# Head norms in groups and biases added by VectorE in the first attention of a two-block network

## The chip, the cores and the metric

One core of one Trainium2 chip runs the whole kernel in one launch. The metric is the device time in microseconds, as the median of several executions. The core has TensorE (matrix products, results in eight banks of PSUM), VectorE, ScalarE, GpSimd and SyncE, each with its own program in order; they hand work to each other by semaphores.

## The reference

Two blocks of two layers each, on 512 tokens of width 1024 in float32. The change lies in the first layer, an attention with two kinds of heads:

```python
def attn_layer(h, w_in, w_out, relpos_table, q_norm_a, k_norm_a, q_norm_b, k_norm_b, sinks):
    qa, ka, va, qb, kb, vb = jnp.split(h @ w_in, cuts, axis=-1)
    qa = rmsnorm(heads(qa, H_A), q_norm_a)
    ka = rmsnorm(heads(ka, H_A), k_norm_a)
    idx = jnp.clip(rel_a, -MAX_REL_DIST, MAX_REL_DIST) + MAX_REL_DIST
    bias_a = relpos_table.astype(jnp.float32)[:, idx][:, None]
    oa = band_attention(qa, ka, heads(va, H_A), A_PREV_CHUNKS, bias_a, None)
    qb = rmsnorm(heads(qb, H_B), q_norm_b)
    kb = rmsnorm(heads(kb, H_B_KV), k_norm_b)
    bias_b = -slopes * abs(rel_b)
    ob = band_attention(qb, kb, heads(vb, H_B_KV), B_PREV_CHUNKS, bias_b, sinks)
    return jnp.concatenate([oa, ob], axis=-1) @ w_out
```

Heads are 64 wide. The eight a heads see all earlier tokens in chunks of 64 and have a bias read from a table by distance. The eight b heads share two key and value heads, see the two chunks before their own, have a bias linear in the distance (ALiBi) and a sink in the maximum and the sum. `rmsnorm` over the 64 of a head is the head norm.

## The kernel before

Activations lie transposed, features on partitions and 512 tokens along the free dimension. A weight matrix comes in slabs of 8 blocks of 128x128 (512 KB). SyncE loads a slab, ScalarE rounds it (`half`, L2054, w_hi), GpSimd subtracts for the remainder (L546, w_lo), and TensorE makes three matmuls for each block of 128x128: w_hi by xh, w_hi by xl, w_lo by xh (L725 to L727). Four slabs are in flight.

`attn_in` has 18 chunks of 128 output columns (144 blocks in all): 13 are normed (`NORMED`: queries and keys) and 5 are values (`VALUES`). The attention itself runs in 32 steps m, four query tiles t of 128 tokens for each of eight pairs of heads; the pairs 0 to 3 are b heads (ALiBi), 4 to 7 are a heads (`is_rel`). Each step has three slots f; `attn_fed` says how many blocks TensorE has done by each slot (9 in 6 slots, after 34 ahead of the steps), and `attn_at` in which slot a chunk's parts stand. The four engines walk the same grid of steps and slots.

Of a step, TensorE makes `score(m)` (two heads at once in the two halves of the array, L766, then the bias by further matmuls into the same bank: one of bf16 for ALiBi, L781; two of a Toeplitz table times the flipped identity, L774 and L776, and the mask, L778, for a heads). VectorE takes the maximum (`peak`, L1893), ScalarE the exponential (`powers`, L2456). One step later TensorE turns the probabilities (`turn`, L790) and ScalarE copies them (`copied`, L2470). Two steps later TensorE multiplies by the values (`outputs`, L809, which waits for b_ol of the step before), ScalarE scales (`weighed`, L2479, b_tok), TensorE turns the result into bank 6 (`turn_out`, L815), ScalarE rounds it (`upper`, L2486, oh) and VectorE subtracts (`low`, L1915, ol). The output projection `attn_out` then runs over all of oh and ol (L609 to L611).

A normed chunk is evicted by VectorE (`evict`, L1875), squared by ScalarE (L2436), summed over each head by a matmul with head_ones, a block matrix that also spreads the sum over the 64 rows of its head, into bank 7 (`finish`, L752); ScalarE takes the root there (L2447), VectorE the reciprocal of 128x512 (L1882) and the scaled product (L1885). A value chunk is turned through bank 7 (L748, L2444).

At the start ScalarE's queue issues the loads of the activations, the constants (cst), the bias table's rows (rel_row), the sinks and the memory tokens (m_in). The table is scaled and split in upper and lower parts (L1856, L1857, L2491, L1921), written to DRAM, and GpSimd reads it back as 128 shifted rows (`load_rel`, 16 loads of 320 KB, four heads at a time). VectorE casts masks_b, head_ones and alibi_b out of cst (L2006 to L2008), and TensorE waits for cst_ready after chunk 0.

Of the kernel before, what the change touches and what calls it, by code (L numbers as in the profile page):

```python
# [30 lines left out]
P = 128  # L31
S = 512
# [49 lines left out]
CONSTS = [("masks", 3 * P), ("head_ones", P), ("alibi", 8 * 256)]  # L82
# [73 lines left out]
def build(nc, A, out, stages=ALL):  # L156
# [4 lines left out]
    with ExitStack() as ctx:  # L161
# [60 lines left out]
        b_q = sb("b_q", [P, 6, S])  # L222
        b_k = sb("b_k", [P, 4, S])
        b_v = sb("b_v", [P, 4, S])
        b_pt = sb("b_pt", [P, 4, S])
        b_tok = sb("b_tok", [P, 2, P])
        b_stat = sb("b_stat", [P, 6, 64])
        alibi_b = sb("alibi_b", [P, 8, 256], BF16)
        head_ones = sb("head_ones", [P, P])
        sink_c = sb("sink_c", [P, 8])  # L230
        flip = sb("flip", [P, P])
        flip_r = sb("flip_r", [P, P], F32R)
        rel_h = sb("rel_h", [P, 4, 640], F32R)
        rel_l = sb("rel_l", [P, 4, 640], F32R)
        b_prob = nc.alloc_sbuf_tensor_at("b_prob", [P, 4, S], F32, offset=m_hi_at)
        cursor[0] = arena
        rel_row = sb("rel_row", [8, 767])
        rel_row_h = sb("rel_row_h", [8, 767], F32R)
        rel_row_l = sb("rel_row_l", [8, 767], F32R)
        cst = sb("cst", [P, NCST])  # L240
        rel_dram_h = nc.dram_tensor("rel_upper", [8, 767], F32R)
        rel_dram_l = nc.dram_tensor("rel_lower", [8, 767], F32R)
# [68 lines left out]
        def col(name, c=0):  # L311
# [22 lines left out]
        q_raw, q_sq, q_sum, q_root, q_rec, q_ready = (  # L334
            sem(n) for n in ("q_raw", "q_sq", "q_sum", "q_root", "q_rec", "q_ready"))
# [9 lines left out]
        cst_in, cst_ready, rel_in, rel_ready, rel_out = (  # L345
            sem(n) for n in ("cst_in", "cst_ready", "rel_in", "rel_ready", "rel_out"))
        rel_hi = sem("rel_hi")
        sink_in, flip_done = sem("sink_in"), sem("flip_done")
        rel_buf = [sem(f"rel_buf{h}") for h in range(4)]
# [23 lines left out]

        def attn_fed(x):

            return min(18 * KD, 34 + 9 * (x + 1) // 6) if x >= 0 else 34

        def attn_at(c, extra):

            x = 0  # L380
            while attn_fed(x) < min(KD * (c + 1) + extra, 18 * KD):
                x += 1
            return x + (1 if KD * (c + 1) + extra > 18 * KD else 0)

        def step_bank(m, half):

            return bank[2 + 2 * (m % 2) + half]

        VALUES = (1, 8, 11, 14, 17)
        NORMED = [c for c in range(18) if c not in VALUES]  # L390
        UNITS = {}

        def norm_slot(c):
# [2350 lines left out]
```

## Time and profile before

| | us |
|---|---|
| median of 3 runs | 3249.08 |
| lowest and highest | 3249.03, 3249.24 |
| the profiled execution | 3255.58 |
| its span, first to last instruction | 3253.7 |
| TensorE busy | 3085.4 (95%) |
| VectorE, ScalarE, GpSimd busy | 1516.7, 1305.3, 1186.2 |

The profile is of one execution, which took 6.5 us more than the median. "Busy" is the time in which an engine had an instruction; matmuls are pipelined and overlap in the record. Where a row has an idle time in brackets, the name behind the arrow is what released the instruction. PEclk is the clock granted to TensorE, 1.00 for 2.4 GHz and 0.50 for 1.2 GHz. The attention lies between 13.5 and about 343 us of the span, its output projection included.

### The profile page before, as it was taken

The page shows a single profiled execution, that of the slowest core. Times are in us where ns is not written, and L with a number is a line of the kernel's source. Part 1 is how long each engine was busy: PE and PEld are TensorE (multiplying, and loading weights), DVE is VectorE, ACT ScalarE, POOL GpSimd, SP SyncE. Part 2 cuts the span into 40 slices and gives each one's busy share as a digit, 9 for nine tenths or more (in the row PEclk, how much of TensorE's full clock was granted, in tenths as well). Part 3 has the DMA queues.
Part 4 walks back from the last instruction along what each step waited for, and adds up shares of the span by engine and source line. Part 5 has one row for each costly group of instructions (what it writes and reads, how often), then busy time and mean ns, then how long its engine had stood idle before and what let it go on. Part 6 is the DMA issues. An engine that isn't in the chain of part 4 may idle for free.

```text
span 3253.7 us, 40002 instructions
## 1 busy us (share of the span) xinstructions
PE 3085.4 (95%) x13798; PEld 2401.8 (74%) x13798; DVE 1516.7 (47%) x2136; ACT 1305.3 (40%) x2061; POOL 1186.2 (36%) x511
## 2 busy tenths in 40 slices
PE   6899999998998899999999999999989999899998
PEld 4566788876675578888866777888867787778886
DVE  5542555327615744553269534332257763333222
ACT  4663444333335534443322534443233343344432
POOL 3121444443342034444432532444432254144443
PEclk9997999999998999999999999999999999999999
DMA  4120323332220022323311322323321132122232
GB/s 151 39 78 22 95 90 97 97 99 75 84 91 7 1 72 91 96 90 100 101 59 59 117 72 60 95 91 96 102 79 59 59 117 85 45 91 92 95 97 90
DMA packets 74459, 263.18 MB, mean 81 GB/s; under 512 B 8664, under 2 KB 8928, under 8 KB 74096
## 3 DMA queue, kind: packets, MB, share of 16 engines
q1 hardware_dynamic: 68400, 249.07, 24.6%
q10 hardware_dynamic: 3648, 7.46, 0.6%
q0 software_dynamic: 2304, 5.24, 0.6%
q8 instruction: 65, 1.06, 0.1%
q14 instruction: 42, 0.34, 0.0%
HBM read 259.59 MB, written 2.15 MB: 80 GB/s over the span
## 4 chain that ended last, share of the span: by engine, by line
PE 45%; issue 34%; POOL 14%; DVE 5%; ACT 2%; DMA 0%; POOLq 0%; ACTq 0%; DVEq 0%; SPq 0%
POOL w_lo L546 14%; PE bank L609 11%; PE bank L610 11%; PE bank L611 11%; PE bank L1108 1%; PE bank L1056 1%; PE bank L1057 1%; PE bank L1058 1%; DVE bank L1882 1%; PE bank L1238 1%; DVE bank L1786 1%; PE bank L1241 1%; PE bank L685 0%; PE bank L725 0%; PE bank L726 0%
## 5 line engine op out<-in xcount | busy, mean ns | idle before, releaser
L546 POOL TENSOR_TENSOR w_lo<-w_raw,w_hi 128x1024 fp32r<-128x1024 f32 x475 | 1144.8, 2412 | 1891.2 <-ACT w_hi L2054 1891.2
L2054 ACT ACTIVATE w_hi<-w_raw 128x1024 fp32r<-128x1024 f32 x475 | 501.1, 1056 | 724.9 <-DMA w_raw<-w_glu_out 156.7
L609 PE MATMUL bank<-xh,w_hi 128*128 128x512 f32 x1864 | 745.5, 400 | 18.0 <-POOL w_lo L546 13.4
L610 PE MATMUL bank<-xl,w_hi 128*128 128x512 f32 x1864 | 740.8, 397 | 0.0
L611 PE MATMUL bank<-xh,w_lo 128*128 128x512 f32 x1864 | 740.4, 397 | 0.0
L609 PEld LDWEIGHTS bank<-xh,w_hi 128*128 128x128 f32 x1864 | 352.1, 189 | 113.2 <-POOL w_lo L546 19.5
L610 PEld LDWEIGHTS bank<-xl,w_hi 128*128 128x128 f32 x1864 | 352.1, 189 | 86.3 <-issue 1.7
L611 PEld LDWEIGHTS bank<-xh,w_lo 128*128 128x128 f32 x1864 | 352.2, 189 | 85.9
L1343 DVE TENSOR_TENSOR xt<-bank,xt 128x512 f32 x72 | 49.8, 692 | 505.6 <-PE bank L611 505.6
L611 PE MATMUL bank<-hh,w_lo 128*128 128x512 f32 x704 | 279.1, 396 | 0.0
L609 PE MATMUL bank<-hh,w_hi 128*128 128x512 f32 x704 | 279.1, 396 | 0.0
L610 PE MATMUL bank<-hl,w_hi 128*128 128x512 f32 x704 | 279.1, 396 | 0.0
L1969 DVE TENSOR_TENSOR f_u<-bank,rstd 128x512 f32<-128x512 f32 x88 | 60.9, 691 | 274.2 <-PE bank L611 274.2
L2547 ACT ACTIVATE hh<-f_h 128x512 f32 x88 | 55.6, 632 | 257.8 <-DVE f_h L1972 257.8
L610 PEld LDWEIGHTS bank<-hl,w_hi 128*128 128x128 f32 x704 | 132.6, 188 | 32.3
L609 PEld LDWEIGHTS bank<-hh,w_hi 128*128 128x128 f32 x704 | 132.6, 188 | 32.3
L611 PEld LDWEIGHTS bank<-hh,w_lo 128*128 128x128 f32 x704 | 132.6, 188 | 32.3
L1972 DVE TENSOR_TENSOR f_h<-f_y,f_u 128x512 f32<-128x512 f32 x88 | 150.7, 1712 | 8.5 <-DVE f_u L1969 2.7
L1786 DVE SCALAR_TENSOR_TENSOR bank<-c_u,cols,bank 128x512 f32<-128x512 f32 x192 | 130.3, 750 | 12.7 <-PE bank L1108 12.2
L1317 DVE TENSOR_TENSOR acc<-acc,sq 128x512 f32<-128x512 f32 x88 | 102.3, 1163 | 71.1 <-ACT sq L2045 71.1
L609 PE MATMUL bank<-oh,w_hi 128*128 128x512 f32 x320 | 129.9, 406 | 2.6 <-DVE ol L1840 2.1
L610 PE MATMUL bank<-ol,w_hi 128*128 128x512 f32 x320 | 128.3, 401 | 0.0
(341 smaller groups left out, 4660.0 us busy)
## 6 DMA issues: line engine op xcount, KB each, us to landing
w_raw<-w_ffn_in SPq DMA_DIRECT2D x88, 512.0 KB, 3.5
w_raw<-w_glu_in SPq DMA_DIRECT2D x88, 512.0 KB, 3.5
w_raw<-w_ffn_out SPq DMA_DIRECT2D x48, 512.0 KB, 3.5
w_raw<-w_glu_out SPq DMA_DIRECT2D x48, 512.0 KB, 3.5
w_raw<-w_ssm_in SPq DMA_DIRECT2D x41, 512.0 KB, 3.5
w_raw<-w_pw SPq DMA_DIRECT2D x24, 512.0 KB, 3.5
w_raw<-w_diff_in SPq DMA_DIRECT2D x24, 512.0 KB, 3.5
w_raw<-w_attn_in SPq DMA_DIRECT2D x18, 512.0 KB, 3.5
```

The lines of the kernel that those rows point to most:

```text
L546: pool.tensor_tensor(w_lo[:, slot, :], w_raw[:, slot, :], w_hi[:, slot, :].bitcast(F32), ALU.subtract).then_inc(w_split, 1)
L609: pe.matmul(b, wh, hi[:, k, 0:n], start=(k == 0), stop=False)
L610: pe.matmul(b, wh, lo[:, k, 0:n], start=False, stop=False)
L611: mm = pe.matmul(b, wl, hi[:, k, 0:n], start=False, stop=last)
L1056: pe.matmul(b, wh, hi[:, k, 0:n], start=(k == 0), stop=False)
L1317: dve.tensor_tensor(acc[:], acc[:], sq[:, j % 2, :], ALU.add).then_inc(x_acc, 1)
L1343: dve.tensor_tensor(row(xt, c), b[:], row(xt, c), ALU.add).then_inc(bank_free, 1)
L1786: ins = dve.scalar_tensor_tensor(conv_bank(p)[:], c_u[:, p % 4, k:k + S], col("dw_w", CONVW * p + k), conv_bank(p)[:], ALU.mult, ALU.add)
L1969: dve.tensor_tensor(f_u[:], bu[:], rstd[:], ALU.mult).then_inc(bank_free, 1)
L1972: dve.tensor_tensor(f_h[:], f_y[:], f_u[:], ALU.mult).then_inc(f_prod, 1)
L2054: act.activation(w_hi[:, slot, :], w_raw[:, slot, :], ACT.Copy).then_inc(w_half, 1)
L2547: act.activation(row(hh, p), f_h[:], ACT.Copy)\
```

## The change

- The 13 normed chunks form seven groups (`GROUPS`). `sums` makes a thin result: for each chunk of a group two rows (one a head) of 32 in bank 7, with a selection matrix `pick`. ScalarE takes the root of 32x512 into acc, VectorE the reciprocal in two halves of 256 columns, in two slots, and `spread` brings it back to 128 rows of bank 7 by a matmul over 32 rows with `heads`.
- The blocks are fed 40 ahead of the steps and then 5 in 4 slots, so that they last into step 27 instead of step 24. The order of the chunks is k, q, v, q.. instead of k, v, q.. at the head.
- The biases are no longer matmuls. `peak` is one VectorE operation per head, which adds the bias (rel_t or alibi_b) in the bank and takes the maximum with the sink as its floor. rel_t comes ready made from the host for all eight heads (128x640 each); GpSimd loads it, one head a slab, scales it by 8 and adds the mask.
- Bank 7 is shared by sums, spreads, value transposes and output transposes in one order (`SHARED`), each waiting for the release of the one before. Outputs are turned, rounded and subtracted once for each pair (128x512) instead of once for each step.
- Buffers for all keys, queries and values, so that no eviction waits for scores. The load of m_in moves from the start to the first feed-forward layer.

```diff
+        VALUES = (2, 8, 11, 14, 17)
+        GROUPS = ((0, 1), (3, 4), (5,), (6, 7), (9, 10), (12, 13), (15, 16))
+        EARLY = (8, 8, 8, 4, 4, 4, 4)
+        SLOT0 = len(EARLY)
         def attn_fed(x):
-            return min(18 * KD, 34 + 9 * (x + 1) // 6) if x >= 0 else 34
+            if x < SLOT0:
+                return sum(EARLY[:x + 1])
+            return min(18 * KD, sum(EARLY) + 5 * (x - SLOT0 + 1) // 4)
...
+        def turn_step(m):
+            return m + 1
+        def output_step(m):
+            return m + 2
+        def group_slot(g):
+            return attn_at(GROUPS[g][-1]) + 1
+        def shared_bank():
+            events = []
+            for g, chunks in enumerate(GROUPS):
+                events.append((group_slot(g), 0, "sums", g))
+                events += [(group_slot(g) + 3 + (i if g else 0), 1, "spread", c) for i, c in enumerate(chunks)]
+            events += [(attn_at(c) + 1, 2, "values", c) for c in VALUES]
+            events += [(slot_of(output_step(NT * pair + NT - 1), 2), 3, "output", pair) for pair in range(8)]
+            return sorted(events)
...
+            def attn_stream(st):
+                for c in range(st.chunks):
+                    if 3 <= c < 11:
+                        pool.dma_start(rel_t[:, c - 3, :], A["rel_t"][c - 3]).then_inc(rel_in[c - 3], 16)
+                    if 6 <= c < 14:
+                        h = c - 6
+                        pool.wait_ge(rel_in[h], 16)
+                        if h == 0:
+                            pool.wait_ge(cst_ready, 2)
+                        pool.tensor_scalar(rel_t[:, h, :], rel_t[:, h, :], 8.0, None, ALU.mult).then_inc(rel_done, 1)
+                        pool.wait_ge(rel_done, 2 * h + 1)
+                        pool.tensor_tensor(rel_t[:, h, S:], rel_t[:, h, S:], masks_b[:, 0, :], ALU.add).then_inc(rel_done, 1)
+                    lower_half(st.slab0 + c)
...
-                    pe.matmul(bank[7][:], head_ones[:], sq[:, 0, :], start=True, stop=True).then_inc(q_sum, 1)
+                def sums(g):
+                    for i, c in enumerate(GROUPS[g]):
+                        pe.wait_ge(q_sq, NORMED.index(c) + 1)
+                        pe.matmul(bank[7][0:32, :], pick[:, 30 - 2 * i:62 - 2 * i], sq[:, i, :], start=(i == 0),
+                                  stop=(c == GROUPS[g][-1]), skip_group_check=True).then_inc(q_sum, 1)
+                def spread(c):
+                    g, i = place_of(c)
+                    pe.wait_ge(q_rec, 2 * g + 2)
+                    pe.matmul(bank[7][:], heads[:, i * P:(i + 1) * P], acc[0:32, :], start=True, stop=True).then_inc(q_bc, 1)
...
+                def output(pair):
+                    pe.wait_ge(b_otok, NT * (pair + 1))
+                    for t in range(NT):
+                        mm = pe.transpose(bank[7][:, t * P:(t + 1) * P], b_tok[:, t, :], ident[:])
+                    mm.then_inc(b_ot, 1)
...
                     if m:
-                        pe.wait_ge(b_ol, m)
+                        pe.wait_ge(b_otok, m)
...
+                def inverse(g, part):
+                    dve.wait_ge(q_root, g + 1)
+                    r = acc[0:32, part * 256:(part + 1) * 256]
+                    dve.reciprocal(r, r).then_inc(q_rec, 1)
...
-                        top = dve.reduce_max(b_stat[:, 0, u:u + 1], step_bank(m, half)[:, 0:nk], AX_X)
+                        top = dve.tensor_tensor_reduce(b, b, bias, 1.0, floor, ALU.add, ALU.max, b_stat[:, 0, u:u + 1])
...
+                def rooted(g):
+                    act.wait_ge(q_sum, normed_in(g + 1))
+                    if g:
+                        act.wait_ge(q_bc, normed_in(g))
+                    act.activation(acc[0:32, :], bank[7][0:32, :], ACT.Sqrt, scale=1.0 / 64, bias=eps[0:32, 0:1])\
+                        .then_inc(q_root, 1)
...
-                dve.tensor_copy(head_ones[:], cst[:, 3 * P:4 * P]).then_inc(cst_ready, 1)
-                dve.tensor_copy(alibi_b[:], cst[:, 4 * P:].rearrange("p (a n) -> p a n", a=8)).then_inc(cst_ready, 1)
+                dve.tensor_copy(pick[:], cst[:, 3 * P:3 * P + 64]).then_inc(cst_ready, 1)
+                dve.tensor_copy(heads[:].rearrange("p (a n) -> p a n", n=64),
+                                ident[0:32, 0:8].unsqueeze(2).broadcast_to([32, 8, 64])).then_inc(cst_ready, 1)
...
+                if s == "ffn0":
+                    act.dma_start(m_in[:], A["memt"]).then_inc(m_landed, 16)
...
-            act.dma_start(m_in[:], A["memt"]).then_inc(m_landed, 16)
```

## Rows read from the trace of the kernel before

**Rows 1.** stretches of the first attention: us from:to, length, busy (x) by engine, clock, DMA

```profile
13.50:57.80 44.30, 32.56 (x114) 22.49 (x114) 30.64 (x30) 19.15 (x26) 19.11 (x14) 0.92 0.51 169
57.80:241.70 183.90, 163.43 (x849) 116.36 (x849) 94.09 (x206) 112.54 (x295) 37.52 (x22) 0.95 0.17 52
241.70:252.60 10.90, 8.62 (x54) 5.60 (x54) 3.17 (x11) 5.24 (x20) 0.00 (x0) 1.00 0.12 46
252.60:298.00 45.40, 39.67 (x164) 30.06 (x162) 8.30 (x27) 15.29 (x52) 0.00 (x0) 0.54 0.00 1
```

**Rows 2.** timeline of the start, ScalarE and its queue: start, us, engine, line, operation

```profile
7.47 0.45 ACTq L2562 DMA_DIRECT2D m_in<-memt  x1
...
8.03 1.28 ACT L2054 ACT_TABLE_LOAD   x1 [8.03 <-issue]
```

**Rows 3.** timeline around the constants' casts, GpSimd and TensorE

```profile
23.48 5.22 POOL L546 TENSOR_TENSOR w_lo<-w_raw,w_hi 128x1024 fp32r<-128x1024 f32 x2 [10.66 <-ACT w_hi L2054]
...
29.97 0.79 PE L725 MATMUL bank<-xh,w_hi 128*128 128x512 f32 x1 [4.64 <-DVE alibi_b L2008]
```

**Rows 4.** timeline ahead of the first scores, ScalarE and TensorE

```profile
51.93 1.06 ACT L2054 ACTIVATE w_hi<-w_raw 128x1024 fp32r<-128x1024 f32 x1 [6.15 <-DMA w_raw<-w_attn_in]
...
57.78 0.59 PE L766 MATMUL bank<-b_k,b_q 64*128 64x128 f32 x4 [4.99 <-DVE b_q L1885]
```

**Rows 5.** timeline of TensorE in a step with no norm chain

```profile
124.63 0.39 PE L781 MATMUL bank<-alibi_b,ident_b 128*128 128x256 bf16 x2
...
124.78 0.48 PE L725 MATMUL bank<-xh,w_hi 128*128 128x512 f32 x1
...
126.26 0.60 PE L748 MATMUL bank<-ident,sq 128*128 128x128 f32 x4
...
126.69 1.00 PE L809 MATMUL bank<-b_v,b_pt 128*128 128x64 f32 x8
...
127.51 0.48 PE L725 MATMUL bank<-xh,w_hi 128*128 128x512 f32 x1
```

**Rows 6.** timeline of a step with a norm chain, TensorE and VectorE

```profile
150.31 1.02 PE L752 MATMUL bank<-sq,head_ones 128*128 128x512 f32 x2
...
151.17 0.60 PE L790 MATMUL bank<-ident,b_prob 128*128 128x128 f32 x4
...
152.06 3.37 DVE L1882 RECIPROCAL bank<-bank 128x512 f32<-128x512 f32 x1 [4.52 <-ACT bank L2447]
...
156.47 1.10 PE L809 MATMUL bank<-b_v,b_pt 128*128 128x64 f32 x8 [1.38 <-DVE ol L1915]
```

**Rows 7.** timeline of TensorE in two steps with no projections, around their biases

```profile
242.36 0.38 PE L774 MATMUL bank<-rel_h,flip_r 128*128 128x256 f32 x1
...
243.13 1.95 PE L809 MATMUL bank<-b_v,b_pt 128*128 128x64 f32 x16
...
246.88 0.45 PE L774 MATMUL bank<-rel_h,flip_r 128*128 128x384 f32 x1
...
247.88 0.61 PE L809 MATMUL bank<-b_v,b_pt 128*128 128x64 f32 x4
```

**Rows 8.** timeline of the tail: an exponential, the last scores, the first output projection

```profile
248.88 0.58 ACT L2456 ACTIVATE b_prob<-bank,b_stat 128x384 f32<-128x384 f32 x1 [2.54 <-DVE b_stat L1897]
...
278.95 2.08 PE L766 MATMUL bank<-b_k,b_q 64*128 64x512 f32 x4
...
297.97 0.77 PE L609 MATMUL bank<-oh,w_hi 128*128 128x512 f32 x1
```

**Rows 9.** groups by line and shape, VectorE: count, busy us, mean ns, idle before

```profile
L1736 DVE RECIPROCAL rstd<-rstd 128x256 f32<-128x256 f32 x8 | 13.8, 1738 | 1.3 <-ACT rstd L2331 1.3
...
L1763 DVE TENSOR_TENSOR bank<-bank,rstd 128x512 f32<-128x512 f32 x8 | 5.5, 693 | 18.2 <-PE bank L1058 18.2
...
L1893 DVE TENSOR_REDUCE b_stat<-bank 128x1 f32<-128x512 f32 x8 | 5.3, 689 | 7.6 <-PE bank L778 7.6
...
L1515 DVE TENSOR_SCALAR a_stat<-a_stat 128x1 f32<-128x1 f32 x64 | 9.8, 154 | 2.2
```

More of the change, by code:

```diff
@@ L344, in build @@
             sem(n) for n in ("a_score", "a_max", "a_exp", "a_prob", "a_turn", "a_pt", "a_pv", "a_oh", "a_ol"))
[L345 to L349, printed above, removed]
+        cst_in, cst_ready, sink_in, sink_ready, rel_done = (
+            sem(n) for n in ("cst_in", "cst_ready", "sink_in", "sink_ready", "rel_done"))
+        rel_in = [sem(f"rel_in{h}") for h in range(8)]
         def score_bank(n, peers):
@@ new lines, in build, with released, place_of @@
+        SHARED = shared_bank()
+        def released(k):
+            _, _, kind, n = SHARED[k]
+            if kind == "sums":
+                return q_root, n + 1
+            if kind == "spread":
+                return q_ready, NORMED.index(n) + 1
+            if kind == "values":
+                return v_ready, 2 + VALUES.index(n) + 1
+            return b_ol, n + 1
+        def place_of(c):
+            g = next(i for i, chunks in enumerate(GROUPS) if c in chunks)
+            return g, GROUPS[g].index(c)
@@ L391, in build, with normed_in @@
+        def normed_in(groups):
+            return sum(len(chunks) for chunks in GROUPS[:groups])
         UNITS = {}
@@ new lines, in output, with events @@
+                def output(pair):
+                    pe.wait_ge(b_otok, NT * (pair + 1))
+                    for t in range(NT):
+                        mm = pe.transpose(bank[7][:, t * P:(t + 1) * P], b_tok[:, t, :], ident[:])
+                    mm.then_inc(b_ot, 1)
+                use = {"sums": sums, "spread": spread, "values": values, "output": output}
+                def events(x):
+                    for k, (at, _, kind, n) in enumerate(SHARED):
+                        if at == x:
+                            pe.wait_ge(*(released(k - 1) if k else (nrm_root, nrm[0])))
+                            use[kind](n)
@@ L757, in score @@
                     if t == 0:
[L758 removed]
+                        pe.wait_ge(q_ready, NORMED.index(7 + 3 * (pair - 4)) + 1 if is_rel(m) else 2 + pair)
                     if m >= 2:
@@ L1865, in evict @@
                             dve.wait_ge(v_turned, v)
+                        dve.wait_ge(q_sum, sum(n < c for n in NORMED))
                         dst = sq[:, 1, :]
```

345 lines of the change are left out of this document (134 added, 211 removed).

## Prediction

> **What bounds the kernel now.** The change touches only the first attention, so I read that stage first in stretches [rows 1], then the waits by line, then the timelines of single steps. The stage has four parts. From 13.5 to 57.8 us the first three and a half weight chunks run alone, and 34 of 144 projection blocks (a block is three matmuls of 512 columns) are done. From 57.8 to 241.7, the steps 0 to 24 carry the other 110 blocks. From 241.7 to 298.0, the steps 25 to 33 have no block left, and then the output projection starts [rows 8]. In the second part TensorE is busy 163.4 of 183.9 us: 20.5 are idle, and a granted clock of 0.95 means that a tenth of the time ran at 1.2 instead of 2.4 GHz, which costs 9.2. So its work there is 154.2 us at 2.4 GHz, and 29.7 are lost. In the last part the clock is 1.00 up to 252.6 and 0.54 after it: TensorE had been busy 8.6 of 10.9 us before it fell. The stage is bound by TensorE's work and, around it, by waits that cost time twice, as idle and as clock.
>
> The waits have a pattern. In a step with a head norm, VectorE's reciprocal of 128x512 takes 3.37 us, and VectorE works in order: behind it stand the scaling, the small subtraction into ol and the maximum. TensorE's weighted sums wait 1.38 us for that ol [rows 6]. In a step without a norm TensorE has no gap [rows 5]. There are eleven such chains in the steps and thirteen in all.
>
> **The front, to the first scores.** ScalarE's first work starts at 8.03 us, just behind its own queue's last issue, the load of m_in at 7.47 [rows 2]. The change takes two issues out of that queue (m_in, moved to ffn0, and rel_row), up to 1.0 us earlier (the m_in issue is 0.45, the other is taken alike), nothing if the first weights had only just landed. In ffn0 the issue stands behind the norm's root, where VectorE's 3.37 us reciprocal covers it; uncovered it would cost 0.45. TensorE then waits until 29.97 for the constants' casts, which share the time with two GpSimd subtractions of 5.22 us together [rows 3]. The cast of head_ones becomes one of 64 columns, and a copy into heads (32x512) is added, at most 0.7 by the 128x512 rows. GpSimd now goes on to its third slab without the wait for rel_out; if a cast has to wait for that subtraction too (5.22/2 = 2.6 us), it costs that. Of the two together I take -0.5, bounds -1.0 and +2.6. The old front lost 6.15 us on a slab that landed at 51.93, behind the burst of sixteen 320 KB bias loads, and TensorE then stood 4.99 us before the scores [rows 4]. The new loads are eight, one for each slab, so I take no such wait (bound: the 6.15 stay). What takes its place is the work: 40 blocks instead of 34 (6 x 0.74 = 4.4, from 1.48 us for two blocks [rows 5]), one more spread pair (2 x 0.86 [rows 6]), one wait between the two spreads (scaling and hand-over, 0.9). Two sums and one set of value transposes stand in the front as now. So score 0 starts at 57.8 - 0.5 - 5.0 + 4.4 + 2.6 = 59.3, against 57.8 now.
>
> **The steps with projections.** Part by part, at 2.4 GHz, from the 154.2 us:
> - Six blocks fewer (110 to 104): -4.4.
> - Biases leave TensorE. For an ALiBi step they take 0.15 (124.63 to 124.78) [rows 5], 16 times 2.4. For a relative step 0.77 with 256 keys and 1.00 with 384 [rows 7], so by the same slope 0.54 and 1.23 with 128 and 512, 3.54 for a pair; two pairs and step 24 give 7.6. Together -10.0.
> - Output transposes: 23 single ones, about 0.1 each (a quarter of 0.43, 126.26 to 126.69), become six groups of four, 0.43 each: 0.
> - Sums: thinner output, the same 512 columns in. No row shows a 32-wide result; the bounds are 0.22 and 0.86, and I take the 0.86 of [rows 6], so 0.
> - Spreads are new: 11 matmuls of 32x512 in these steps, at 0.86: +9.5. The lower end is half of that.
> - Three more steps (25 to 27) come into this part. TensorE was busy 8.6 us in two of them, less 1.8 of bias, and half as much again for the third: about +9.
>
> Sum 158.3 us. On it come the stalls. The eleven chains with a 3.37 us reciprocal become six with two of 1.74 (128x256 [rows 9]; 32 rows save nothing, since the time goes with the columns), placed in different slots, with the spread three slots after the sum. From the end of the sums: root and hand-over 0.9 (151.17 to 152.06 [rows 6]), up to 1.3 for its table (the length of a table load [rows 2] is in that stretch hidden by the wait), 1.74 twice, so 4.4 to 5.7 us. Three slots of TensorE's work (158.3/28/3 = 1.9 each) give 5.7 less the slot's share that lies before the sums, so about 1.2 of stall for each group, 7 in all. The weighted sums now wait for b_otok (ScalarE) and not for ol (VectorE), so nothing on TensorE waits behind the reciprocal but the spreads. Behind the reciprocals on VectorE stands the next maximum, up to 1.7 late; its exponential is wanted by TensorE more than a slot later. Five more for the other waits and some low clock: 12, bounds 3 (almost none) and 29.7 (as much as now). GpSimd gets sixteen more operations, at most 8 x (1.6 + 0.3) us from its 2.6 for 1024 columns; it waits most of the stage, and its slabs are wanted 18 blocks later, so 0. So step 28 starts at 59.3 + 170.3 = 229.6.
>
> **VectorE's bias and maximum in one.** No row has that operation. The nearest are the maximum (0.689 for 512 columns) and an addition from bank to bank (0.693) [rows 9]. Bounds for 512 columns are 0.69 (one pass) and 1.38 (two); I take 0.75, and 0.15 for handing out the maximum, the price of the 128x1 row. That is 0.2 more for each half than now, 0.4 for a step, while one of three small operations of the ALiBi steps goes. VectorE is busy 94 of 184 us [rows 1], so this costs only where the step is a chain, at the end. The Trainium skill, VectorE: DVE Perf Modes, section "Two Vector instructions with no wait between them", says that an operation with an accumulator output is two instructions, the main one and a read of the accumulator. No row here shows one on VectorE; by it the 0.15 is an instruction of its own, and by a single one the tail below would be about 1 us shorter.
>
> **The end.** Only the steps 28 to 31 and the two behind them have no blocks. Steps 25 and 26 now take 4.3 and 5.1 us at 2.4 GHz, with ScalarE waiting 2.54 us for the maximum [rows 8]. Bias out (0.8) and VectorE's extra (0.4) nearly cancel; steps 28, 29, 30 at 3.6, 4.3 and 5.1 give 13.0. Step 31 to the output projection takes 19.0 now, at 1.2 GHz (278.95 to 297.97 [rows 8]); bias goes (2.2 at that clock) and the ol wait goes (0.9), VectorE's extra and the four transposes cost 1.1: 17. I let the clock fall again, in step 30: +1. The tail is 31, bounds 25 (the clock stays) and 40 (it falls at once and VectorE takes two passes).
>
> **Sum.** The output projection starts at 229.6 + 31 = 260.6 instead of 298.0: -37.4 us. What follows is the same program. The profiled execution took 3255.6 with a span of 3253.7, and the median of the runs is 3249.1; I apply the difference to both: 3218.2 for such an execution, and 3211.7 for the median.
>
> **Rivals.**
> - Almost no stall is left and the spreads cost half: stalls 3 instead of 12, spreads -5, tail 27: 9 + 5 + 4 = 18 less, 3194. For it: steps without a norm have no gap now. Against: the shared bank. Chance 0.13.
> - The shared bank takes the reciprocal's place. Sums, spreads, value and output transposes all use bank 7 in one order, and TensorE stands in order at each. There are 33 such uses. If they cost 0.7 us each on average instead of what I allow, the stalls are about 30 and with their clock the result is about 3230. For it: a chain of 4.4 to 5.7 us per group, with TensorE behind it. Against: three slots are left for it. Chance 0.2.
> - Slower. The same place, the handing on of bank 7: at 33 uses the gain of 37 plus the 7 already counted is used up at 44/33 = 1.3 us each. At 2 us each it is 66 - 44 = 22 slower, 3271. The longest wait of TensorE for a norm now is 4.99, and eleven chains with all else cost 29.7, so this needs more loss from six groups than eleven give now. Chance 0.04.
> - It does not do what it says: the stage stays bound as now, because the steps' stalls stay near 30 and the tail runs wholly at 1.2 GHz (40), and the front loses 2.6 more. 37 - 18 - 9 - 3 = 7 of gain are left, 3242; with VectorE dearer, within 0.2%. Chance 0.06.
>
> **Numbers.** The forecast has 0.57 (3201 to 3222). The range reaches into the first two rivals: 3195 to 3230. A measurement of this kernel can tell about 0.2%, 6.5 us. Faster 0.93, same 0.03, slower 0.04.
>
> **What would show it.** Right: score 0 near 59.3 and no wait for a slab ahead of it; steps of some 6.1 us; reciprocals of 1.74, fourteen of them; no wait of the weighted sums for ol; blocks up to step 27; the output projection at 261. Wrong: TensorE waiting before spreads or sums by more than 2 us a group; a bias-and-maximum above 1 us for 512 columns; a low clock before step 28; the first block after the casts later than 32.

## The result and the profile after

The changed kernel takes 3229.11 us, the median of 5 runs (3225.24 to 3234.08), against 3249.03 for the kernel before beside it (5 runs, 3242.79 to 3249.24). The ratio is 0.9944, 95% interval 0.9929 to 0.9958: 18 us faster by the ratio, 20 by the two medians. The forecast was 37.4 us faster (3211.7), with 3230 as the slow end of its range. The direction came out; the size is about half, at the slow end of that range.

The profile after is of an execution of 3225.24 us (span 3223.4), the fastest of the five. Its stage in stretches, as [rows 1]: up to the first scores, up to step 28, and up to the output projection. Columns as there: from:to, length, busy time of TensorE, its weight loads, VectorE, ScalarE and GpSimd, the granted clock, and the DMA columns.

```profile
13.50:59.97 46.47, 39.13 (x133) 25.95 (x131) 28.06 (x28) 17.75 (x25) 22.87 (x15) 0.93 0.35 115
59.97:237.29 177.32, 163.18 (x818) 108.19 (x817) 81.78 (x242) 102.45 (x286) 47.04 (x29) 0.98 0.15 45
237.29:266.05 28.76, 22.72 (x125) 18.50 (x125) 6.16 (x27) 12.07 (x40) 1.13 (x1) 0.72 0.06 19
```

Score 0 starts at 59.97 us (59.3 forecast), step 28 at 237.29 (229.6), the output projection at 266.05 (260.6; [rows 8] have 297.97). What a stretch loses to the clock is its length times what the clock lacks to 1.00: 177.3 x 0.02, some 3.5 us; added up from short windows, as all such losses below, it is 3.4. So the steps hold 163.2 - 3.4 = 159.8 us of work at 2.4 GHz, 14.1 idle and 3.4 of clock. 158.3 of work was forecast and 12 for the other two together.

The start and the casts, timeline of the same kernel, as [rows 2, 3]:

```profile
6.94 1.28 ACT L2091 ACT_TABLE_LOAD   x1 [6.94 <-issue]
...
22.38 5.22 POOL L564 TENSOR_TENSOR w_lo<-w_raw,w_hi 128x1024 fp32r<-128x1024 f32 x2 [10.66 <-ACT w_hi L2091]
22.87 2.53 DVE L2041 CAST masks_b<-cst 128x384 bf16<-128x384 f32 x1
25.32 2.33 DVE L2042 COPY pick<-cst 128x64 f32<-128x64 f32 x1
```

ScalarE begins 1.1 us earlier, as both issues out of its queue promised (up to 1.0). VectorE's operations, by line and shape (count, busy us, mean ns, idle before), as [rows 9]:

```profile
L1911 DVE RECIPROCAL acc<-acc 32x256 f32<-32x256 f32 x14 | 24.0, 1726 | 14.6 <-ACT acc L2481 14.6
L1946 DVE CUSTOM_DVE_ANT_0 bank<-bank,alibi_b,sink 128x256 f32<-128x256 f32 x24 | 10.5, 479 | 11.7 <-PE bank L828 11.7
L1946 DVE DVE_READ_ACCUMULATOR2_ANT b_stat<- 128x1 f32 x64 | 8.9, 140 | 0.0
...
L1946 DVE CUSTOM_DVE_ANT_0 bank<-bank,rel_t 128x512 f32<-128x512 f32 x8 | 5.4, 715 | 12.3 <-PE bank L828 12.3
```

Fourteen reciprocals of 32x256 take 1726 ns each, close to what the 1738 of [rows 9] for 128x256 said. The bias and maximum in one take 715 ns for 512 columns and 140 for the accumulator (0.75 and 0.15 taken). The Trainium skill, VectorE: DVE Perf Modes, section "Two Vector instructions with no wait between them", says that an operation with an accumulator output is two instructions; this trace agrees, with 64 reads of 140 ns in rows of their own.

What TensorE waited for between 55 and 300 us (total, times, longest):

```profile
PE bank L828 <- ACT b_pt L2521: 10.1, 11, 3.0
PE bank L793 <- DVE acc L1911: 6.1, 4, 3.1
PE bank L804 <- ACT b_tok L2531: 1.3, 2, 0.7
```

L793 is `spread`, waiting for the reciprocals; L828 `score`, waiting for the last probabilities' copy. Inside the steps (up to 237.3) the first of the three is 6.3 us in nine waits and the second is whole. No matmul of L856, the weighted sums, waits for VectorE any more, as [rows 6] had it for L809. The tail of the changed kernel, timeline of TensorE, as [rows 8]:

```profile
250.40 2.08 PE L828 MATMUL bank<-b_k,b_q 64*128 64x512 f32 x4 [3.01 <-ACT b_pt L2521]
...
256.53 2.79 PE L856 MATMUL bank<-b_v,b_pt 128*128 128x64 f32 x12 [0.88 <-ACT b_pt L2521]
...
265.31 1.09 PE L804 MATMUL bank<-ident,b_tok 128*128 128x128 f32 x4 [0.70 <-ACT b_tok L2531]
266.05 0.78 PE L655 MATMUL bank<-oh,w_hi 128*128 128x512 f32 x1
```

### The profile page after: what moved, and what is told of

Same layout as the page of the kernel before. It is cut to its first block, busy times and chain, and to the rows that moved or that the text cites. A ratio compares the mean times of both kernels' runs of the same rounds, so it can differ in the third digit from the quotient of the medians.

```text
span 3223.4 us, 39788 instructions
## 1 busy us (share of the span) xinstructions
PE 3068.6 (95%) x13696; PEld 2381.8 (74%) x13696; DVE 1499.1 (47%) x2159; ACT 1285.8 (40%) x2020; POOL 1199.1 (37%) x517
## 3 DMA queue, kind: packets, MB, share of 16 engines
q8 instruction: 64, 1.05, 0.1%
## 4 chain that ended last, share of the span: by engine, by line
PE 45%; issue 34%; POOL 14%; DVE 4%; ACT 2%; POOLq 0%; ACTq 0%; DMA 0%; DVEq 0%; SPq 0%
POOL w_lo L592 14%; PE bank L655 11%; PE bank L656 11%; PE bank L657 11%; PE bank L1144 1%; PE bank L1092 1%; PE bank L1093 1%; PE bank L1094 1%; PE bank L1274 1%; PE bank L771 1%; DVE bank L1822 1%; PE bank L772 1%; PE bank L773 1%; PE bank L731 1%; DVE acc L1911 0%
## 5 line engine op out<-in xcount | busy, mean ns | idle before, releaser
L592 POOL TENSOR_TENSOR w_lo<-w_raw,w_hi 128x1024 fp32r<-128x1024 f32 x457 | 1100.6, 2410 | 1760.0 <-ACT w_hi L2091 1760.0
L655 PE MATMUL bank<-xh,w_hi 128*128 128x512 f32 x1864 | 745.3, 400 | 18.8 <-POOL w_lo L592 14.2
```

What stands on the lines that cost most here:

```text
L592: pool.tensor_tensor(w_lo[:, slot, :], w_raw[:, slot, :], w_hi[:, slot, :].bitcast(F32), ALU.subtract).then_inc(w_split, 1)
L655: pe.matmul(b, wh, hi[:, k, 0:n], start=(k == 0), stop=False)
```

## The experiments

All ratios are to the kernel before, run beside each kernel. "Spread" is L793, "idle" and "clock" are what TensorE loses in a stretch; its "work" is its busy time less the clock's loss.

**Both kernels again.** One profile of each is thin ground for a difference of 20 us.

> The kernel before, unchanged, for a second profile. Between the two profiles at hand the output projection of the first attention starts 32 us earlier after the change (298.0 to 266.0) and the spans differ by 30, but the medians differ by 20. Theory A, the first profile of before was an unusual execution: its low clock inside the first attention (five falls of 3.4 us in the steps, 48 us in the tail) is more than usual; then this profile shows fewer falls, a projection start of 286 to 292 us, and a time near 3245 to 3249. Theory B, the attention always gains 32 and the rest of the program gives some back after the change: then this profile shows a start near 298 again with a span near its own median, so 6 us less behind 298 than the first profile had (2955.7). The ratio to itself is 1.000 within 0.2%.

> The changed kernel, unchanged, for a second profile; its first one came from its fastest execution (3225.2, others up to 3234.1). Theory A, low clock inside the attention differs by execution: a slower profile shows its extra time ahead of 266 us, with more falls of the clock there. Theory B: the start of the output projection stays at 266 within 1 us, and the extra time lies behind it. Ratio to before 0.994 within 0.002.

Before: 3247.37 us (12 runs, 3242.7 to 3254.81), ratio 0.9998 [0.9988, 1.0008]. After: 3228.22 (5 runs, 3226.69 to 3237.75), ratio 0.9950 [0.9938, 0.9963]. The spread within one program goes with the clock: over the whole span the changed kernel had 0.977 at 3226.69 and 0.974 at 3237.75, the one before 0.977 at 3242.70 and 0.974 at 3254.81. A clock of 0.003 less is 10 us of such a span. Stretches of the new profile of before (up to score 0, to step 25, to the output projection), then of the changed kernel (to score 0, to step 28, to the output projection):

```profile
13.50:57.30 43.80, 31.98 (x112) 22.04 (x112) 30.65 (x30) 19.15 (x26) 19.08 (x14) 0.96 0.54 171
57.30:241.34 184.04, 163.41 (x849) 116.58 (x849) 94.16 (x206) 112.57 (x295) 37.50 (x22) 0.95 0.18 52
241.34:292.46 51.12, 43.41 (x215) 32.78 (x216) 11.33 (x38) 20.39 (x72) 0.00 (x0) 0.71 0.03 10
```

```profile
13.50:60.51 47.01, 39.06 (x134) 25.80 (x132) 27.97 (x27) 17.70 (x25) 22.88 (x15) 0.93 0.35 115
60.51:244.65 184.14, 170.82 (x818) 113.07 (x817) 80.42 (x242) 102.96 (x286) 47.07 (x29) 0.94 0.14 43
244.65:271.45 26.80, 20.75 (x124) 16.42 (x125) 6.16 (x27) 12.09 (x40) 1.13 (x1) 0.81 0.06 20
```

Of the two theories the first fits for the kernel before: its second profile starts the output projection at 292.5. Three things follow. First, the tail of before is 51.1 us here and 56.3 in [rows 1]: its clock came back to 1.00 for 10 us in between (0.71 over the tail against 0.54 in the last row of [rows 1]). The forecast took its tail from one execution, 6.5 us above the median, that had the worse case. Second, from the start of the output projection to the end the program is the same but for the load of m_in, and it took 2955.7 and 2953.5 us in the two profiles of before and 2957.3 and 2953.5 in the two of the change: it moves by 4 us by itself, so a difference of a few us between two profiles isn't yet one between two kernels. Third, the changed kernel's steps take 184.1 us with the clock at 0.94 and 177.3 at 0.98, with the same waits (13.3 and 14.1 us idle). Where the low clock lay in the slower of these two, the one just shown:

```profile
67.40:70.60 3.20, 0.16 (x1) 0.00 (x0) 3.20 (x3) 1.03 (x1) 0.82 (x2) 0.94 0.15 62
70.60:80.40 9.80, 9.74 (x19) 4.42 (x20) 3.76 (x15) 2.55 (x8) 5.11 (x4) 0.50 0.12 33
...
118.00:124.80 6.80, 6.80 (x20) 4.61 (x20) 2.33 (x6) 2.19 (x9) 2.00 (x2) 0.50 0.10 20
138.50:141.90 3.40, 3.40 (x16) 3.00 (x15) 0.66 (x6) 1.59 (x8) 1.62 (x2) 0.50 0.00 0
```

TensorE was nearly idle from 67.4 to 70.6 (the spread of the first group in the steps, 3.10 us), and then ran at 1.2 GHz for 9.8 us, busy throughout. At 118.0 the waits ahead were short (0.71 us in the step before), and the other profile, with the same wait (0.72), had no fall there. Behind the wait of 3.10 us both profiles have a low clock, one for 10 us and the other for 7. The Trainium skill, TensorE: Matmul & The Clock Gate, section "A second HAM failure mode: psum-queue depth-cycling", says that in a bf16 kernel which cycles through its PSUM banks, short idles between groups of matmuls make the clock go up and down. The falls at 118.0 and 138.5, behind waits of 0.71 and 1.72 us, are of that kind, and their absence in the other profile is not explained by it; no run here changes how the banks are used.

**Fewer blocks a slot alone, in the kernel before.** Does the longer cover of the steps pay by itself?

```diff
-            return min(18 * KD, 34 + 9 * (x + 1) // 6) if x >= 0 else 34
+            return min(18 * KD, 34 + 8 * (x + 1) // 6) if x >= 0 else 34
```

> The kernel before with one part of the change alone: its 110 blocks in the steps go 8 to 6 slots instead of 9 to 6, so that they last into step 27 instead of 24. My sum has the three later steps without blocks as the tail's gain, mostly by the clock: before, 45 us run at 0.54. If the low clock of the tail is the main thing that the change removes, this alone gives 8 to 15 us (ratio 0.995 to 0.9975), and the tail from step 28 is about 31 to 35 us. If the tail is bound by its chain, blocks moved there only fill gaps: also a gain, but of the idle in the steps 25 to 27, 2 to 5 us (0.9985 to 0.9995).

3238.61 us, ratio 0.9971 [0.9962, 0.9981]: 9 us. Its stretches, to step 28 and to the output projection:

```profile
57.19:249.84 192.65, 171.39 (x923) 121.03 (x923) 97.97 (x221) 118.98 (x322) 37.41 (x22) 0.98 0.17 50
249.84:280.79 30.95, 25.83 (x142) 19.41 (x143) 6.47 (x23) 13.02 (x45) 0.00 (x0) 0.77 0.04 16
```

Steps 0 to 27 and the tail together take 223.6 us instead of 235.2. Nearly all of that is clock: 11.1 us are lost instead of 23.5 (3.9 in the steps and 7.2 in the tail, against 8.5 and 15.0), while the idle is 26.4 instead of 28.3. The steps are as idle as before (21.3 us against 20.6), and still lose less than half as much to the clock.

**The reciprocal alone, and the biases alone, in the kernel before, and both.** The change shortens the chain and takes the biases off TensorE; which of the two pays?

```diff
-                    dve.reciprocal(bank[7][:], bank[7][:]).then_inc(q_rec, 1)
+                    dve.reciprocal(bank[7][:, 0:256], bank[7][:, 0:256]).then_inc(q_rec, 1)
```

```diff
-                        pe.matmul(step_bank(m, half)[:, 0:nk], q, k, start=True, stop=False, skip_group_check=True)
...
-                            pe.matmul(b[:, 0:nk], ident_b[:], alibi_b[:, 4 * half + pair, 256 - nk:256], start=False, stop=True,
-                                      skip_group_check=True).then_inc(b_score, 1)
+                        pe.matmul(step_bank(m, half)[:, 0:nk], q, k, start=True, stop=True, skip_group_check=True)\
+                            .then_inc(b_score, 1)
```

> The kernel before with the head norms' reciprocal taken over 256 of 512 columns (the other half is left at the root, so the second half of the tokens is scaled wrongly; same instructions otherwise). It halves the one instruction that I named as the source of the stalls: 3.37 to 1.74 us, 13 times, 21 us in all, 11 of them in the steps. In the two profiles of before the steps 0 to 24 take 184.0 us with 20.6 idle and 8.5 lost to the low clock. If VectorE's reciprocal is what TensorE waits for, at least half of the 18 us goes from the steps: idle near 11, ratio 0.995 to 0.997. If the waits come from elsewhere in the in-order chain (ScalarE's part, table loads), idle falls by under 3 and the ratio is above 0.9985.

> The kernel before without its bias matmuls (biases and masks are left out of the scores; all loads stay). My sum took 10.0 us of TensorE's work out of the steps 0 to 24 and some 7 at the low clock out of the tail. If TensorE's work is the bound, the steps are 10 us shorter and the start of the output projection 14 to 17 us earlier: ratio 0.9945 to 0.996. If the steps are bound by chains, idle takes the place of the work, work falls by 10 but the steps by under 5: ratio above 0.9975.

> The kernel before with the bias and mask matmuls left out and the reciprocal over 256 of its 512 columns (half of the tokens keep the root instead of its inverse; the biases are missing from the scores, so nothing that comes after is the reference's). Apart, the first gave 4 us and the second 16. If the work that leaves TensorE is worth nothing while chains through VectorE and ScalarE set the steps, and is worth its length once they are shorter, the two together give more than 20: some 27, ratio 0.9910 to 0.9925. If the clock takes what the work gives (an emptier engine falls to 1.2 GHz more often), they give 20 or less: 0.9935 to 0.9955.

| left out of the kernel before | us | ratio | gain |
|---|---|---|---|
| half of each reciprocal | 3230.78 | 0.9951 [0.9937, 0.9966] | 16 |
| all biases and masks on TensorE | 3242.98 | 0.9985 [0.9975, 0.9996] | 3 to 5 |
| both | 3222.36 | 0.9920 [0.9903, 0.9936] | 25 |

The steps 0 to 24 and the tail, first with half reciprocals, then without biases, then with neither:

```profile
56.53:224.42 167.89, 157.56 (x849) 113.92 (x849) 78.10 (x206) 112.23 (x295) 37.52 (x22) 0.98 0.19 57
```

```profile
56.89:235.42 178.53, 155.51 (x763) 109.97 (x763) 94.32 (x206) 112.71 (x295) 37.45 (x22) 0.95 0.18 54
235.42:284.12 48.70, 39.93 (x174) 29.62 (x174) 10.87 (x38) 20.50 (x72) 0.00 (x0) 0.61 0.03 10
```

```profile
55.49:216.15 160.66, 147.69 (x763) 105.31 (x763) 78.22 (x206) 112.18 (x295) 37.52 (x22) 0.99 0.21 60
```

Halving the reciprocal takes 16.2 us off the steps without touching TensorE's work: idle 20.6 to 10.3, clock 8.5 to 3.4. Each of the eleven norms loses 1.6 us of reciprocal (3.37 to 1.77), 17.6 us in all, so rather more than half of what VectorE saves was idle of TensorE, and the clock gave 5.1 on top. The weighted sums' wait for ol, which the prediction had named, falls from 6.1 to 0.6 us in the steps; the output transposes' wait for b_tok, which it had not, stays (6.8 to 6.3). Taking 8.7 us of work out of the steps gave 5.5 (178.5 against 184.0); idle grew by 2.4 and the clock's loss by 0.8. In the tail some 7 us of work went and 2.4 of time: the clock there was 0.61 instead of 0.71. I had expected more of the biases (a miss). With half reciprocals under it, the same removal is worth 8 to 10 us by the medians (3230.78 to 3222.36), but the intervals of the two, 1 to 8 and 3 to 17 us, overlap widely, and by the profiles it is the same: the output projection starts 8.3 us earlier without the biases (292.5 to 284.1) and 8.7 earlier with half reciprocals under it (272.9 to 264.2). The idle grows alike as well, by 2.4 and by 2.7 us. So it isn't shown that removed work is worth more once the chain is shorter. The 27 us that I had worked out for both was 25.

**The spreads one slot later, in the changed kernel.** If TensorE waits at L793 for the reciprocal, a later spread should find it done.

```diff
-                events += [(group_slot(g) + 3 + (i if g else 0), 1, "spread", c) for i, c in enumerate(chunks)]
+                events += [(group_slot(g) + (4 if g else 3) + (i if g else 0), 1, "spread", c) for i, c in enumerate(chunks)]
```

> The changed kernel with the spreads of all groups but the first one slot later (four after the sums instead of three). I priced a group's stall before the spread at 1.2 us; the profiles show 3.1, 0.98, 0.72, 0 to 0.4 and 1.34: 6.5 in all, and a fall of the clock of 7 to 10 us behind the first. If the spread is too early, the first wait becomes 1.5 or less and the others go: idle less by 4 to 5, and the clock does not fall at 70 us: ratio 0.991 to 0.9935. If VectorE's reciprocals only move with the slots, nothing changes: 0.9945 to 0.9955.

3220.07 us (3219.45 to 3222.05), ratio 0.9917 [0.9899, 0.9935]: 8 us better than the change. TensorE's waits for the reciprocal, and the steps:

```profile
PE bank L793 <- DVE acc L1911: 2.4, 1, 2.4
```

```profile
60.06:231.85 171.79, 162.83 (x817) 108.50 (x817) 81.82 (x241) 102.20 (x286) 47.94 (x29) 0.98 0.15 46
```

Four waits of 6.1 us became one of 2.4; the steps take 171.8 us, idle 9.0 and clock 3.4. Against the slower of the two profiles of the change, 4.3 us of idle and 8.3 of clock are gone; against the faster 5.1 and nothing. Two signs of the expectation missed: the first wait is 2.4 us and not 1.5 or less, and the clock is still low behind it, from about 72 to 80 us.

**Half reciprocals in the changed kernel.** The same wait, from its other side.

```diff
-                    r = acc[0:32, part * 256:(part + 1) * 256]
+                    r = acc[0:32, part * 256:part * 256 + 128]
```

> The changed kernel with each reciprocal of the head norms over 128 of its 256 columns (half of the tokens keep the root instead of its inverse). If what the spreads wait for is the reciprocals' own length, as the waits of 3.10, 0.98, 0.71 and 1.36 us before spreads say, they shrink by 1.74 each where they are that long (0.87 times 2), the steps become some 4 us shorter and the clock falls less often: as good as the spreads one slot later, ratio 0.991 to 0.993. If the spreads wait for something else that VectorE does first, it stays at 0.9945 to 0.9955.

3221.74 us, ratio 0.9923 [0.9906, 0.9940]. The steps:

```profile
61.11:233.41 172.30, 162.93 (x818) 108.13 (x817) 72.67 (x242) 102.58 (x286) 47.06 (x29) 0.98 0.14 46
```

172.3 us, idle 9.4, clock 3.5: shortening the reciprocal and moving the spread away from it do the same. The wait is the reciprocals'. It is 1.5 us here, once, and the clock behind it is low as before (71 to 80 us): what brings that fall, in every profile of the changed kernel, stays open.

**ScalarE copies the probabilities ahead of its norm work.** The other large wait, scores for b_pt, might go if ScalarE did that copy first in its slot.

```diff
+                        for j in range(BM):
+                            if f == 1 and turn_step(j) == m:
+                                copied(j)
...
-                            if f == 1 and turn_step(j) == m:
-                                copied(j)
```

> The changed kernel with one order changed on ScalarE: in a step's middle slot the copy of the turned probabilities comes before that slot's squares and roots, not after. In both profiles of after, TensorE stands 1.0 to 1.7 us before the scores of steps 5, 11, 19 and 24 for that copy, which stands behind a square that waits for VectorE's eviction of a chunk that TensorE has only just finished. I priced no such wait. If this is the cause, these waits go: 4 to 5 us of idle in the steps (of 13.7), and the falls of the clock behind them (at 118 and 138 us in the second profile) become rarer: ratio to before 0.991 to 0.9935 against 0.995 of the change. If the square is late instead and holds the sums, the waits only move: ratio 0.994 to 0.996.

3241.35 us (10 runs, 3238.57 to 3245.11), ratio 0.9985 [0.9975, 0.9995]: 11 to 13 us slower than the change, where I had expected it faster. One group's chain, timeline of ScalarE, VectorE and TensorE, in the changed kernel run again, and then with the copy ahead:

```profile
83.50 0.66 PE L837 MATMUL bank<-ident,b_prob 128*128 128x128 f32 x4
...
84.11 0.68 ACT L2481 ACTIVATE acc<-bank,eps 32x512 f32<-32x512 f32 x1
...
84.82 1.74 DVE L1911 RECIPROCAL acc<-acc 32x256 f32<-32x256 f32 x1 [3.07 <-ACT acc L2481]
...
87.66 1.73 DVE L1911 RECIPROCAL acc<-acc 32x256 f32<-32x256 f32 x1
...
89.54 1.09 PE L793 MATMUL bank<-acc,heads 32*128 32x512 f32 x2 [0.98 <-DVE acc L1911]
```

```profile
84.31 0.65 PE L837 MATMUL bank<-ident,b_prob 128*128 128x128 f32 x4
...
84.79 0.66 ACT L2521 ACTIVATE b_pt<-bank 128x256 f32<-128x256 f32 x2 [1.65 <-PE bank L837]
85.47 1.28 ACT L2481 ACT_TABLE_LOAD   x1
86.76 0.68 ACT L2481 ACTIVATE acc<-bank,eps 32x512 f32<-32x512 f32 x1
...
87.47 1.74 DVE L1911 RECIPROCAL acc<-acc 32x256 f32<-32x256 f32 x1 [5.10 <-ACT acc L2481]
...
90.32 1.73 DVE L1911 RECIPROCAL acc<-acc 32x256 f32<-32x256 f32 x1
...
92.19 2.04 PE L793 MATMUL bank<-acc,heads 32*128 32x512 f32 x2 [3.40 <-DVE acc L1911]
```

As the kernel has it, ScalarE loads the root's table (82.81 to 84.09) while TensorE still makes the sums, and takes the root 0.6 us after TensorE's next matmul starts (84.11 after 83.50). With the copy ahead, the copy waits for the transposes (84.79), the table load of 1.28 stands behind it in the open, and the root comes 2.45 us after (86.76 after 84.31). The spread waits 3.40 instead of 0.98. TensorE's waits between 55 and 300 us, and the steps:

```profile
PE bank L793 <- DVE acc L1911: 10.5, 5, 3.4
PE bank L828 <- ACT b_pt L2521: 7.0, 8, 3.0
```

```profile
61.12:255.14 194.02, 177.38 (x817) 116.69 (x816) 83.16 (x241) 103.51 (x286) 48.18 (x29) 0.90 0.13 41
```

The scores' wait shrank by 2 to 3 us and the spreads' grew by 4.3. There are as many table loads as before (six for the root and seven for the exponential in the steps), so it is their place and not their number. Idle is 16.6 instead of 13.3, but the clock is 0.90 and takes 18.5 instead of 11.7: of the 9.9 us that the steps are longer, two thirds are clock.

**Dummy matmuls in the tail of the changed kernel.** What does the low clock at the end cost? Eight matmuls in each of the steps 28 to 32, into a bank that nobody reads.

```diff
+                def fill(n):
+                    pe.wait_ge(bank_free, BANKS + st.chunk0 + 17)
+                    for _ in range(n):
+                        pe.matmul(bank[0][:, P:4 * P], ident_b[:], masks_b[:], start=True, stop=True, skip_group_check=True)
...
+                        if 28 <= m <= 32 and f == 2:
+                            fill(8)
```

> The changed kernel with eight small bf16 matmuls of 384 columns into an unused bank at the end of each of the steps 28 to 32, as padding. In the profile after, the clock is at 1.2 GHz from 249.7 to 270.2 us. If idle is what lets it fall, this keeps it at 2.4 GHz; TensorE's work there at 1.2 GHz is some 14 us plus four at the head of the projection, so the gain is up to 9 us (the chain's other parts, VectorE and ScalarE, stay), less the padding that does not fit into gaps, 1 to 3: a gain of 5 to 8 us against the change (ratio to before 0.991 to 0.993). If the clock falls all the same, the padding costs 3 to 6.

3222.54 us, ratio 0.9929 [0.9914, 0.9943]: 5.7 us better than the change. The tail takes 26.5 us with a clock of 1.00, where the two profiles of the change have 28.8 and 26.8; behind it, at the head of the projection, the first of them loses 2.1 us to the clock, the second and this one nothing. So its profile shows 0.3 to 4.4 us of the 5.7. With this and the later spreads together:

> The changed kernel with both edits that helped: the spreads one slot later and the eight dummy matmuls in each of the steps 28 to 32. If the two act on different stretches (the steps, by a shorter wait and a clock that stays up; the tail, by its clock), the gains of 8 and 5.7 us add: ratio to the kernel before 0.990 to 0.9915, 3214 to 3217, the output projection near 257 and the clock at 1.00 in the tail. If the clock falls somewhere else in return, as often as it is held here, it stays at the 0.9917 of the later spreads alone.

3215.22 us (3214.50 to 3219.72), ratio 0.9903 [0.9886, 0.9920]: 32 us faster than the kernel before and 13 faster than the change. The two gains, 8 and 5.7, add within what the runs can tell. The steps and the tail of that kernel:

```profile
59.71:231.51 171.80, 162.82 (x818) 108.40 (x817) 81.62 (x241) 102.20 (x286) 47.96 (x29) 0.98 0.14 46
231.51:257.98 26.47, 22.46 (x164) 16.89 (x165) 6.42 (x27) 12.05 (x40) 0.19 (x1) 1.00 0.07 21
```

The tail's clock is 1.00, and it takes 26.5 us in spite of 40 matmuls more.

## Why the prediction missed the size

The profiled execution of the changed kernel nearest to its median (3226.7, output projection at 271.5) against that of before nearest to its own (3247.8, at 292.5) gives 21.0 us. The way from 37.4 to 21.0:

| | forecast | measured | us of gain |
|---|---|---|---|
| the forecast | | | 37.4 |
| output projection of before | 298.0 | 292.5 | -5.5 |
| score 0 of the changed kernel | 59.3 | 60.5 | -1.2 |
| steps 0 to 27 | 170.3 | 184.1 | -13.8 |
| tail | 31 | 26.8 | +4.2 |
| sum | | | 21.1 |

With the faster profile of the change the steps are 177.3 (-7.0 instead of -13.8), the tail 28.8 and the gain 26.4, in spite of nearly the same time of the whole kernel.

**The sum of the work was right.** 158.3 us of TensorE's work in the steps was forecast; 159.1 and 159.8 were measured. Two of its terms were off and nearly cancel with others: a spread takes 1.02 to 1.05 us from its start to that of the next matmul (112.95 to 113.97 in the first profile), not 0.86, some 2 us in eleven; and the biases of the steps 0 to 24 were 8.7 us of work, not 10.0. Right were the start (6.9 us for ScalarE's first work, against 8.0), the reciprocals' 1.7 us and their number, the price of the combined bias and maximum, the last blocks in step 27, and the outputs' freedom from VectorE. Sixteen more operations on GpSimd cost TensorE no wait.

**The step that failed is the "five more for the other waits and some low clock".** The other term of the stalls, about 7 us of waiting before the spreads, is what was measured: 6.1 and 6.2, in four waits instead of six. The rest was 7.1 us of idle and 11.7 us of clock in the execution of 3226.7, 18.8 instead of 5 (in the fastest, 8.0 and 3.4). Of that idle, 5.4 us (6.3 in the fastest) are eight or nine waits of the scores for ScalarE's copy b_pt, which had no price of their own; the idle alone was more than the whole term. And the clock's loss, 9.2 us in the steps of before [rows 1], was let go almost entirely, without a row that said so. The runs show no rule by which it goes with the idle. The later spreads and half reciprocals have 3.4 and 3.5 of clock with 9.0 and 9.4 of idle; the change has 3.4 or 11.7 with 14.1 or 13.3; the kernel before with fewer blocks a slot has 3.9 with 21.3. With the later spreads the steps take 171.8, 1.5 from the forecast.

The record of all executions says how much hung on this. The forecast counted 30 us of clock before (9.2 and 45.4 x 0.46 [rows 1]) and 9.5 after (8.5 of the 17 at 1.2 GHz, and 1), with some of the five: 15 to 20 of its 37.4 us were clock. What an execution loses to the clock is its span times what its mean clock lacks to 1.00, and the mean over executions is 78 us in the kernel before (59 executions) and 77 in the changed one (10). So on average the change got back next to nothing from the clock, and its 18 to 20 us are less idle and less work. Up to the output projection, the profile of 3226.7 has 12.8 us less idle than the second of before, 3.5 less work and 4.7 less clock.

**The second failed step is the base.** The tail of before was read as 45.4 us at 0.54 [rows 1] from one profile that stood 6.5 us above the median, and the prediction moved both kernels by that difference. 5.5 of it belonged to before alone, nearly all of it in the tail: its long low clock lay where the change takes steps away, so the excess was counted as gain.

**The tail was priced too high.** Steps 28 to 30 took 13.1 (13.0 forecast). From step 31 to the output projection I had 17, at 1.2 GHz throughout, and 1 more for the end of step 30. It took 15.65 in the first profile, at 1.2 GHz throughout, and 13.7 in the second, where the clock came back 3 us ahead of the projection.

**The rivals.** "The shared bank takes the reciprocal's place" named the result, 3230, but not its cause, so the hit is luck. There are no 33 dear uses of bank 7: TensorE waited for its release at four spreads, and once each for VectorE's release of another use (0.8 and 0.4) and for ScalarE's root (1.0). What it had right is the place, the chain of 4.4 to 5.7 us with TensorE three slots behind it; at the third step that chain took 6 us, from the sums' end near 83.5 to the second reciprocal's end at 89.4, because VectorE puts the next maximum (1.2 us) between the two halves. "Almost no stall" (3194) failed by its idle, 14 us against 3, and by the clock; "slower" and "does not do what it says" did not come.

**Where the gain comes from.** In the kernel before, the half reciprocal gives 16 us, fewer blocks a slot 9, the missing biases 3 to 5 alone and 8 to 10 with the half reciprocal. Against these stands what the change spends: eleven spreads in the steps are some 11.4 us of TensorE's time. One more wait went that the prediction hadn't listed, and in the kernel before it was the largest in the steps. TensorE's waits in the first profile of before, 57.8 to 252 us:

```profile
PE bank L815 <- ACT b_tok L2479: 8.9, 10, 1.7
PE bank L809 <- DVE ol L1915: 6.1, 5, 2.2
```

L815 is `turn_out`, each step's output transpose, behind ScalarE's scaling. The change turns outputs once a pair, and in its steps there is no such wait; in the tail it is 1.3 us. No run tests that part alone, nor the larger buffers, so the shares of the gain are not separated.

How much of each run's gain was clock, from all its executions (us; mean loss to the clock over the whole span, 78 in the kernel before):

| run | gain by the medians | loss to the clock | executions |
|---|---|---|---|
| the change | 20 | 77 | 10 |
| fewer blocks a slot | 9 | 68 | 9 |
| half of each reciprocal | 16 | 71 | 5 |
| no biases | 3 | 88 | 10 |
| both | 25 | 78 | 4 |
| the change, spreads later | 26 | 70 | 4 |
| the change, half reciprocals | 26 | 74 | 4 |
| the change, copy first | 5 | 87 | 10 |
| the change, dummy matmuls | 25 | 66 | 4 |
| the change, spreads later and dummy matmuls | 32 | 63 | 4 |

Fewer blocks a slot gained by the clock alone. Without the biases, 10 us more went to the clock, which took most of what the missing work gave. Of the 8 us of the later spreads some 7 are clock, and of the 11 to 13 us that the copy cost about 10. What stays open is what decides whether the clock falls at one and the same wait: two executions of one program differ in it, and no edit here separates them.

## What to carry to other kernels

Give the low clock a term of its own, with a range, and not a share of the waits: here one program lost 3.4 or 11.7 us to it in the same steps, and runs with the most idle were not those with the lowest clock. Sum the waits by what each waits for, also those that are not in the pattern. Take the state of the kernel before from several executions, and above all the stretch which the change removes, since a bad clock there is counted as gain. And don't count removed work as time: 8.7 us of work taken out of the steps gave 5.5, the rest came back as idle and low clock.

## What the runs showed of the hardware

- The clock. One program with the same waits lost 3.4 or 11.7 us to 1.2 GHz in the same 28 steps; runs of one kernel spread over 11 to 12 us, in step with the mean granted clock (0.974 to 0.977). Forty dummy matmuls in five steps held it at 1.00, and the kernel was 5.7 us faster.
- A VectorE operation on 8 columns took as long as the GpSimd subtraction beside it. Changed kernel run again, timeline of both engines:

```profile
27.51 0.41 DVE L2043 COPY heads<-ident 32x512 f32<-32x512 f32 x1
...
29.08 2.54 DVE L1892 TENSOR_SCALAR sink<-sink_c 128x8 f32<-128x8 f32 x1
29.20 2.39 POOL L564 TENSOR_TENSOR w_lo<-w_raw,w_hi 128x1024 fp32r<-128x1024 f32 x1
```

The copy of 512 columns, with GpSimd issuing a DMA beside it, took 0.41 us; the scaling of 8 columns took 2.54, ending with GpSimd's 2.39. The small casts of the start (2.53, 2.33), beside the two subtractions of 5.22, are of the same kind: here the time was the neighbour's and not the size's.
- A reciprocal costs by its columns alone: 1726 ns for 32x256, 1738 for 128x256 [rows 9], 3.37 us for 128x512 [rows 6], so thinning it over partitions saved nothing by itself, and fewer columns did: thirteen of 512 columns became fourteen of 256.
